# Memory tokens turned by VectorE's 32 by 32 transposes in place of TensorE's, with the memory weights' rows read in the order that this leaves

## What is computed

```python
def rms_norm(x, g):
    xf = x.astype(jnp.float32)
    y = xf * lax.rsqrt(jnp.mean(xf * xf, axis=-1, keepdims=True) + EPS)
    return (y * g.astype(jnp.float32)).astype(x.dtype)
...
        mem_n = rms_norm(mem, norm_mem_src[l])        # mem: 256 x 2048
...
    kv = (mem_n @ w_kv).reshape(b, m, 2, MEM_HEADS, MEM_HEAD_DIM)   # w_kv: 2048 x 1024
    k, v = kv[:, :, 0], kv[:, :, 1]
```

## Time and profile before

| | us |
|---|---|
| median of 3 runs | 1361.85 |
| lowest, highest | 1360.79, 1362.06 |
| span of the profiled execution | 1359.5 |
| PE busy | 1003.1 |
| DVE busy | 579.6 |
| ACT busy | 300.6 |
| POOL busy | 52.5 |

### The profile page before, as it was taken

How to read it: one execution, slowest core, us unless ns; L and a number is a source line. 1 busy time by engine, 2 the same in 40 slices (tenths; PEclk the granted TensorE clock), 3 DMA queues, 4 the chain that set the end, 5 groups by cost and what they waited for, 6 DMA issues and landing times.

```text
span 1359.5 us, 20738 instructions
## 1 busy us (share of the span) xinstructions
PE 1003.1 (74%) x8580; PEld 605.0 (45%) x8580; DVE 579.6 (43%) x1119; ACT 300.6 (22%) x521; POOL 52.5 (4%) x108
## 2 busy tenths in 40 slices
PE   8999999999999976566655566655566655566656
PEld 7888888888888532222222222222222222222222
DVE  5545566786557553223332223332223332223323
ACT  5654457664455200000000000000000000000002
POOL 1300001222000000000000000000000000000001
PEclk9999999999999998778777778787777787777879
DMA  7866663238878999999999999999999999999997
GB/s 245 276 194 184 174 177 122 101 128 261 292 272 304 354 429 420 434 432 430 432 432 432 432 432 432 432 432 432 432 432 432 432 432 432 432 432 432 432 424 294
DMA packets 71220, 481.15 MB, mean 354 GB/s; under 512 B 9543, under 2 KB 19917, under 8 KB 57998
## 3 DMA queue, kind: packets, MB, share of 16 engines
q1 hardware_dynamic: 70684, 478.22, 87.1%
q10 hardware_dynamic: 306, 2.11, 0.4%
q0 software_dynamic: 192, 0.31, 0.2%
HBM read 478.52 MB, written 2.10 MB: 354 GB/s over the span
## 4 chain that ended last, share of the span: by engine, by line
PE 51%; DMA 45%; SPq 1%; DVE 1%; issue 1%; ACT 0%; DVEq 0%; ACTq 0%
DMA gu<-in_w_up 41%; PE ps L1028 10%; PE ps L576 8%; PE ps L578 8%; PE ps L577 8%; PE ps L1083 5%; DMA down<-in_w_down 4%; PE ps L1007 2%; PE ps L1040 1%; PE ps L556 1%; PE ps L827 1%; PE ps L828 1%; PE ps L829 1%; PE ps L754 1%; SPq L441 0%
## 5 line engine op out<-in xcount | busy, mean ns | idle before, releaser
L1028 PE MATMUL ps<-gu,xe 128*32 128x256 f32 x3968 | 285.7, 452 | 305.1 <-DMA gu<-in_w_up 304.6
L2096 DVE TENSOR_TENSOR x_sum<-ps,x_sum 128x512 f32<-128x512 f32 x240 | 149.1, 684 | 508.6 <-PE ps L1040 508.6
L1028 PEld LDWEIGHTS ps<-gu,xe 128*32 128x32 f32 x3968 | 140.4, 129 | 468.4 <-DMA gu<-in_w_up 327.8
L1580 DVE TENSOR_TENSOR w_lo<-w_raw,w_hi 128x1024 fp32r<-128x1024 f32 (+1 forms) x137 | 164.9, 1209 | 122.5 <-ACT w_hi L1201 119.2
L576 PE MATMUL ps<-w_hi,a_hi 128*128 128x512 f32 (+1 forms) x468 | 183.7, 393 | 0.0
L577 PE MATMUL ps<-w_lo,a_hi 128*128 128x512 f32 (+1 forms) x468 | 179.8, 384 | 0.0
L578 PE MATMUL ps<-w_hi,a_lo 128*128 128x512 f32 (+1 forms) x460 | 176.9, 385 | 0.0
L1201 ACT ACTIVATE w_hi<-w_raw 128x1024 fp32r<-128x1024 f32 (+1 forms) x137 | 141.7, 1039 | 131.8 <-PE ps L578 116.1
L1499 ACT ACTIVATE sg<-ps 128x128 f32<-128x128 f32 x31 | 8.6, 278 | 654.5 <-PE ps L1028 654.5
L1083 PE MATMUL ps<-down,act_t 128*32 128x512 f32 x976 | 112.6, 602 | 6.2 <-DMA down<-in_w_down 6.2
L577 PEld LDWEIGHTS ps<-w_lo,a_hi 128*128 128x128 f32 x468 | 88.0, 188 | 16.4
(11 more groups left out here) (341 smaller groups left out, 866.0 us busy)
## 6 DMA issues: line engine op xcount, KB each, us to landing
down<-in_w_down SPq DMA_DIRECT2D x29, 4096.0 KB, 22.7
gu<-in_w_gate SPq DMA_DIRECT2D x28, 4096.0 KB, 31.6
gu<-in_w_up SPq DMA_DIRECT2D x28, 4096.0 KB, 40.9
w_raw<-in_w_in SPq DMA_DIRECT2D x56, 512.0 KB, 4.2
w_raw<-in_w_out SPq DMA_DIRECT2D x32, 512.0 KB, 4.4
gu<-in_w_up SPq DMA_DIRECT2D x18, 512.0 KB, 6.0
w_raw<-in_w_mem_kv SPq DMA_DIRECT2D x16, 512.0 KB, 3.4
down<-in_w_down SPq DMA_DIRECT2D x13, 512.0 KB, 15.3
```

Source lines behind the costliest of these rows:

```text
L1028: mm = pe.matmul(ps[5][j * SLOTS:(j + 1) * SLOTS, 0:2 * P].rearrange("s (m f) -> s m f", m=2), xe[:, k, :], gu[side][:, :, k, j * P:(j + 1 ...
L1580: ve.tensor_tensor(w_lo[:, u % RING, :, 0:n], w_raw[:, u % RING, :, 0:n], w_hi[:, u % RING, :, 0:n], ALU.subtract).then_inc(S("w_split"), 1)
L2096: ins = ve.tensor_tensor(x_sum[:, t, cols], ps[g][:, :], (x_res if first else x_sum)[:, t, cols], ALU.add)
```

## The change

- The tokens are loaded by four DMAs on ACT's queue, one for each quarter of the columns: partitions 32q to 32q+31 get columns 512q to 512q+511 of all 256 tokens, eight tokens per partition, in pieces of 2 KB (`mem_quads`).
- DVE transposes each of the eight 128 by 512 slices in place, as sixteen columns of 32 by 32 blocks whose elements lie 16 apart (64 bytes). Partition p then holds features 16p to 16p+15. Four of these instructions stand in chunk SB_V, four in SB_V + 1 (`turn_mem`).
- The unit loads of the memory weights read rows 16p + k on partition p, in pieces of 2 KB as before; the gain of the memory norm is loaded by a DMA of its own straight into `g_t` in that order, and the PE transpose of gains has 70 rows.
- PE's 32 transposes of `mem_sb` go. `a_hi` and `a_lo` are written by ACT and DVE from SBUF, reading with the 64-byte step (`mem_heads`, `mem_rest`).
- The squares become eight ACT instructions of 512 elements, four behind chunk SB_K and four behind SB_K + 1. POOL spreads them over a 128 by 256 tile with four added instructions (three small ones make `quad_eye`), PE sums across partitions with two matmuls of one column ahead of the latent chunks, DVE copies the sums out of PSUM, and POOL's norm of the memory moves ahead of the heads.
- The semaphore `counted` becomes a second count of `ranked`; other counts and gain columns are renumbered.

```diff
@@ load of the weights, of the gains
             if MEM_K <= c <= MEM_V:
-                return [cols(w_mem_kv, (c - MEM_K) * UN)]
+                return [w_mem_kv[0, :, (c - MEM_K) * UN:(c - MEM_K + 1) * UN].rearrange(
+                    "(p k) n -> p k n", k=KD)[:, i * UK:(i + 1) * UK, :]]
...
+                sp.dma_start(g_t[:, 70:86], norm_mem_src[0].rearrange("(p k) -> p k", k=KD)).then_inc(
+                    S("mem_loaded"), 16)
@@ tensor
             turn(KV_LAT)
             pe.wait_ge(S("turn_copied"), bank0[KV_LAT])
-            pe.wait_ge(S("mem_loaded"), 16)
+            pe.wait_ge(S("mem_spread"), 1)
+            for t in range(TT):
+                mm = pe.matmul(ps[7][:, t:t + 1], mem_spread[:, NJ * t:NJ * (t + 1), :].rearrange(
+                    "p j s -> p (j s)"), ones[:, 0:1], start=True, stop=True)
+            mm.then_inc(S("squares_summed"), 1)
             for n, (c, i) in enumerate(LATENT):
...
-                if n < KD // 2:
-                    split_turn("mem", mem_sb, 2 * n, 2 * n + 2)
@@ scalar
+            def mem_squares(t):
+
+                sc.wait_ge(S("mem_loaded"), 16 * (NJ + 1))
+                for j in range(NJ):
+                    square(mem_quads[:, NJ * t + j, :], chunk_ss[:, t, j:j + 1], mem_junk[:, :])
+                    sq[0] += 1
+                    sc.wait_ge(S("squared"), sq[0])
...
-                    sc.dma_start(mem_sb[:, :, :], mem[0].rearrange("(t p) d -> p t d", p=P)).then_inc(
-                        S("mem_loaded"), 16)
+                    for q in range(NJ):
+                        sc.dma_start(mem_quads[q * QUAD:(q + 1) * QUAD, :, :],
+                                     mem[0, :, q * UN:(q + 1) * UN].rearrange("(j s) f -> s j f", s=QUAD)
+                                     ).then_inc(S("mem_loaded"), 16)
...
+                if SB_K <= c < SB_V:
+                    mem_squares(c - SB_K)
                 if c == SB_K:
...
+            def mem_heads(k):
+
+                if k == 0:
+                    sc.wait_ge(S("w_used"), START[Q_PE])
+                    sc.wait_ge(S("split_turned"), (SPLIT0["mem"] + KD) // 2)
+                sc.activation(a_hi[:, k, :].rearrange("p (j s) -> p j s", s=QUAD), mem_turned[:, k], ACT.Copy,
+                              scale=g_t[:, 70 + k:71 + k]).then_inc(S("split_hi"), 1)
@@ vector
+            def turn_mem(t):
+
+                ve.wait_ge(S("squared"), 3 * TT + NJ * (t + 1))
+                for j in range(NJ * t, NJ * (t + 1)):
+                    tile = mem_quads[:, j, :].rearrange("p (r k) -> p k r", k=KD)
+                    ve.transpose(tile, tile).then_inc(S("split_turned"), 1)
+
             for c in range(Q_LAT, Q_PE):
                 split_w(DONE[c] + RING)
+                if c >= SB_V:
+                    turn_mem(c - SB_V)
...
+            ve.wait_ge(S("squares_summed"), 1)
+            ve.tensor_copy(sums[:, SS_MEM:SS_MEM + TT], ps[7][:, 0:TT]).then_inc(S("sums_made"), 1)
             for n, (c, i) in enumerate(LATENT):
                 split_w(POS[(c, i)] + RING)
                 if n < KD // 2:
-                    split_rest("mem", 16, k_from=2 * n, k_to=2 * n + 2)
+                    mem_rest(2 * n)
+                    mem_rest(2 * n + 1)
```

More of the change, by code:

```diff
@@ L36 @@
 SLOTS = 32
+QUAD = 32
 NJ = P // SLOTS
@@ L109 @@
         _b = len(SPLIT_BANK)
-        SPLIT_BANK.append(6 + _b % 2 if _name == "mem" else 4 + _b % 4)
+        SPLIT_BANK.append(None if _name == "mem" else 4 + _b % 4)
 def bank_before(b):
@@ L168, in layer @@
         g_nat_at = at[0]
-        g_nat = place("g_nat", [86, P])
+        g_nat = place("g_nat", [70, P])
         g_t = place("g_t", [P, 86])
@@ L201, in layer @@
         c_kv = place("c_kv", [P, TT, KV_RANK + ROPE])
-        mem_junk = place("mem_junk", [P, D], offset=km_at)
-        mem_sb = place("mem_sb", [P, TT, D], offset=o_at)
+        mem_junk = place("mem_junk", [P, UN], offset=km_at)
+        mem_spread = place("mem_spread", [P, TT * NJ, QUAD], offset=km_at + 2048)
+        quad_eye = place("quad_eye", [P, QUAD], offset=km_at + 3072)
+        mem_quads = place("mem_quads", [P, TT * NJ, UN], offset=o_at)
+        mem_turned = mem_quads[:, :, :].rearrange("p j (s k) -> p k j s", k=KD)
         cq_hi = place("cq_hi", [P, 4, SEQ], F32R, offset=k_at)
@@ L356, in load_small @@
             def load_small():
-                for gain, r0, rows in ((norm_mem_src, 16, 16), (norm_mem_x, 32, 16),
-                                       (norm_q_lat, 48, 4), (norm_kv_lat, 52, 2), (norm_mla_out, 54, 8),
-                                       (norm_sb_out, 62, 8), (norm_ffn, 70, 16)):
+                for gain, r0, rows in ((norm_mem_x, 16, 16), (norm_q_lat, 32, 4), (norm_kv_lat, 36, 2),
+                                       (norm_mla_out, 38, 8), (norm_sb_out, 46, 8), (norm_ffn, 54, 16)):
                     sp.dma_start(g_nat[r0:r0 + rows, :], gain[0].rearrange("(k p) -> k p", p=P)
                                  ).then_inc(S("gains_loaded"), 16)
+                sp.dma_start(g_t[:, 70:86], norm_mem_src[0].rearrange("(p k) -> p k", k=KD)).then_inc(
+                    S("mem_loaded"), 16)
                 for t in range(TT):
@@ L379, in early_piece @@
                     sp.wait_ge(S("out_lo"), KD)
-                    sp.wait_ge(S("sums_made"), 1)
+                    sp.wait_ge(S("sums_made"), 2)
                 if n < 8:
@@ L663, in _ @@
                 if i == 3:
-                    pe.wait_ge(S("gains_loaded"), 7 * 16)
-                    pe.transpose(ps[3][:, 0:86], g_nat[:, :], ident[0:86, 0:86]).then_inc(
+                    pe.wait_ge(S("gains_loaded"), 6 * 16)
+                    pe.transpose(ps[3][:, 0:70], g_nat[:, :], ident[0:70, 0:70]).then_inc(
                         S("gains_turned"), 1)
@@ L805, in _ @@
                 if q == 1:
-                    pe.wait_ge(S("sums_made"), 1)
+                    pe.wait_ge(S("sums_made"), 2)
                 split_turn("memx", x_res, 4 * (q - 1), 4 * q)
@@ L997, in rank_all @@
                 pe.matmul(ps[3][:, 0:EXPERTS], ones[:, :], sel[:, EXPERTS:TT * EXPERTS], start=False,
-                          stop=True).then_inc(S("counted"), 1)
+                          stop=True).then_inc(S("ranked"), 1)
             def gather(n):
@@ L1284, in _ @@
             sc.wait_ge(S("gains_turned"), 2)
-            sc.activation(g_t[:, 16:86], ps[3][:, 16:86], ACT.Copy).then_inc(S("gains_copied"), 1)
+            sc.activation(g_t[:, 16:70], ps[3][:, 16:70], ACT.Copy).then_inc(S("gains_copied"), 1)
             sc.wait_ge(S("gains_copied"), 2)
@@ L1319, in _ @@
                     chunk_copy(c, lambda t: v_sb[:, t, n0:n0 + UN], SS_X)
+                if SB_K <= c < SB_V:
+                    mem_squares(c - SB_K)
                 if c == SB_K:
-                    split_head("q", 48, hi=cq_hi)
+                    split_head("q", 32, hi=cq_hi)
                 if c == SB_K + 1:
[L1323 to L1328, removed]
+                    split_head("kv", 36, hi=ckv_hi)
+            def mem_heads(k):
[4 more added lines that the diff above has]
+                              scale=g_t[:, 70 + k:71 + k]).then_inc(S("split_hi"), 1)
             for n, (c, i) in enumerate(LATENT):
@@ L1332, in _ @@
                 if n < KD // 2:
-                    split_head("mem", 16, START[Q_PE], k_from=2 * n, k_to=2 * n + 2)
+                    mem_heads(2 * n)
+                    mem_heads(2 * n + 1)
                 if POS[(c, i)] + 1 < DONE[c]:
@@ L1685, in _ @@
                              ALU.max).then_inc(S("angles"), 1)
+            def turn_mem(t):
[3 more added lines that the diff above has]
+                    ve.transpose(tile, tile).then_inc(S("split_turned"), 1)
             for c in range(Q_LAT, Q_PE):
                 split_w(DONE[c] + RING)
+                if c >= SB_V:
+                    turn_mem(c - SB_V)
                 if c == SB_K + 1:
-                    split_rest("kv", 52, hi=ckv_hi, lo=ckv_lo)
+                    split_rest("kv", 36, hi=ckv_hi, lo=ckv_lo)
                 if SB_Q <= c - 1 < SB_V:
@@ L1692, in _ @@
                     if c == SB_K:
-                        split_rest("q", 48, hi=cq_hi, lo=cq_lo)
+                        split_rest("q", 32, hi=cq_hi, lo=cq_lo)
                     if c - 1 == SB_K + 1:
@@ L1706, in _, with mem_rest @@
             copy_turned(KV_LAT)
+            def mem_rest(k):
+                ve.wait_ge(S("split_hi"), SPLIT0["mem"] + k + 1)
+                ve.scalar_tensor_tensor(
+                    out=a_lo[:, k, :].rearrange("p (j s) -> p j s", s=QUAD), in0=mem_turned[:, k],
+                    scalar=g_t[:, 70 + k:71 + k],
+                    in1=a_hi[:, k, :].rearrange("p (j s) -> p j s", s=QUAD), op0=ALU.mult,
+                    op1=ALU.subtract).then_inc(S("split_lo"), 1)
+            ve.wait_ge(S("squares_summed"), 1)
+            ve.tensor_copy(sums[:, SS_MEM:SS_MEM + TT], ps[7][:, 0:TT]).then_inc(S("sums_made"), 1)
```

(21 more changed lines are left out.)

20 lines of the change are left out of this document (7 added, 13 removed).

## The result

The changed kernel is **slower**: 1362.84 us (median of 20 runs) against 1360.56 us of the kernel before in the same series, ratio 1.0017 with a 95% interval of 1.0011 to 1.0023. That is 2.3 us more, where 2.65 less was forecast; the time lies outside the stated range. The difference is 0.17%, clear of noise but under the 0.2% that the prediction took as the least it could tell from no change.

What follows compares the result with a forecast made beforehand. PE was taken to bound the kernel until about 474 us, then mostly DMAs of expert weights. Span 1359.5 - 3.1 + 0.45 = 1356.85, with the median 2.35 higher, gave 1359.2 us; 8-in-10 range 1358.2 to 1361.2.

Steps and rivals of the forecast that it cites:

- the early load: Four token DMAs from 53 us, landing by 89 us, first read at 116.6 us: nothing, up to 0.5 us lost.
- The cushion I took from ACT's roundings: Behind the early load's issue: three more issues, 1.2 us on ACT, against three weight units of 2.72 us each.
- PE's gain: Latent chunks: removed transposes save 3.5 us, two one-column matmuls cost 0.4 us; 3.1 us less if PE is never starved.
- The transposes: DVE in SB_V and SB_V + 1: 1.07 us each from a stepped write, four in 3.9 us, or 2.5 to 5.3.
- ACT's and DVE's stepped reads: After SB_V + 1's transposes: two heads 0.73 us, `mem_rest` as before or 0.18 more; PE waits 0.45 us at Q_NOPE + 1.
- rival 1: Step halves DVE and ACT rates: transposes 1.25 us, PE waits 1.9 us, net gain 1.2, 1360.65 us; chance 0.25.
- the later latent units: Weight units after the Q_NOPE + 1 wait: 1 to 4 us in hand when the queues are carried on.
- The base of the time: Span of 1359.5 us for the kernel before, with the runs' median 2.35 us above the profiled span.
- "The same": Outcome of no measurable change, within some 0.2% or 2.7 us; chance 0.53 from part of the forecast plus rivals 1 and 3.
- SB_K, SB_V, POOL, the carry to the end: Squares 3.0 us per chunk and SB_V's transposes hidden, POOL nothing; PE savings before 474 us move everything behind.
- The memory weights' rows: Memory weight loads, same bytes and 2 KB pieces, read where DMA engines are two to three tenths busy; counted within early load.
- The rival on the other side: Rival 2, slower: in-place stepped transposes far slower, starving SB_V and SB_V + 1; at 2 us each, 1366 us; chance 0.08.

Runs made afterwards that it cites:

- the three kernels with the whole change: The changed kernel (1362.84 us), the same with transposes one chunk earlier (1360.22 us), and the same with densely written transposes (1360.94 us), all with the change's original load.
- every fourth partition: Kernel before, its token load cut into four DMAs of 8 KB rows, each to 32 partitions taken every fourth; 1360.47 us, ratio 1.0002.
- copy first: Changed kernel with spread loads, earlier transposes and dense write, ACT copying both Q_NOPE chunks' banks before its next rounding and heads; 1357.79 us, ratio 0.9978.
- the dense-write runs: Transposes write densely into the next slot: on the changed kernel alone 1360.94 us; with spread loads and earlier transposes 1358.49 and 1358.59 us.

## Why the prediction was wrong

- **The step that failed: the early load at "nothing, up to 0.5 us lost".** I asked when the tokens would have to be there (116 us, true: they were) and not what the load does to the transfers beside it. It cost 2.1 us by itself and 1.7 to 2.8 in the three kernels with the whole change. The rows to ask were at hand: the DMA engines' slices at six to eight tenths in the first 100 us, against a ring that holds four units. The cushion I took from ACT's roundings, three units, is a cushion for ACT, not for a transfer of 13.6 us. The issues themselves, 1.9 us more on ACT instead of 1.2, were hidden: every fourth partition issues four at one point too and loses nothing.
- **PE's gain, 3.5 us less 0.4.** Right: with every wait in it mended (copy first), the latent stage is 3.10 us shorter than before. The two small matmuls took 0.45.
- **The transposes.** Forecast 1.07 us each, measured 1.076, four in 4.00. The number was right by luck: I put the extra down to the write, and the dense-write runs show that the write's step costs nothing. The first row that spoke against a read cost, line 2084, reads PSUM.
- **ACT's and DVE's stepped reads.** DVE's 0.68 instead of 0.48 us was the upper bound named. For ACT the sum took the old 0.73 per pair; measured 1.29 and 1.31. This term of the sum was mis-sized by 1.1 us over the two pairs before the split. The wait that came of it all was 1.5 us where 0.45 was forecast; rival 1 had 1.9, and its price for a pair of heads, 1.1, was nearer.
- **The bank at K_NOPE + 1** was not in the working, which gave the later latent units 1 to 4 us in hand: the removed transposes had given ACT the time for its copy. 0.4 us when everything else is mended, 0.9 in the changed kernel.
- **The base of the time.** The sum started from three runs with a median of 1361.85; twenty put the same kernel at 1360.56. A run's time lies 1.7 to 1.8 us above its span wherever both are on record, so the 2.35 us held a difference between executions too. The same 2.65 us off the twenty runs' median is 1357.9: the forecast time was 1.3 us too high for its own terms, and the miss is larger than 1362.84 against 1359.2 shows. "The same", which had chance 0.53, is where 0.17% falls by the prediction's own line, but not by any path that it named. (In the first of the 13 slices PE stands at eight tenths, not nine; nothing hangs on it.)
- **SB_K, SB_V, POOL, the carry to the end**: as forecast. ACT's 3 us of squares are hidden, no PE wait falls in SB_V + 1, and the lateness at 212.7 (2.7 us) arrives at the end as 2.4.
- **The memory weights' rows** read 16 apart: median 3.7 us to land instead of 3.4, hidden.

In sum: -3.05 on PE, +1.7 at Q_NOPE + 1 and +0.9 at K_NOPE + 1 (the gaps between matmuls, less what they are without a wait) make -0.4 in the latent stage; +0.3 before the load and +2.8 by the load in this profile; 2.7, measured 2.4 in the spans and 2.3 in the medians. With the 2.1 us that the load costs by itself the sum is 1.7, inside the interval of the ratio (1.5 to 3.1 us). The rival on the other side had the wrong place: not the transposes, but the load.

## What to carry to other kernels

Work that leaves the critical engine leaves its cushions too: price what the replaced instructions gave time to, and price a transfer by what it does to those that share the engines at that moment, not only by when it must land. A load that must go to 32 neighbouring partitions and shares the DMA engines with a short ring is worth spreading in time: some 12 to 14 us apart, the four cost nothing here. Where VectorE or ScalarE must read with a step, let it be done once, by an instruction that has room, and written densely for the readers behind it. And measure a stretch from an instruction of its own, not from the start of the span.

## What the runs showed of the hardware

- DMAs to 32 neighbouring partitions moved 224 GB/s with the weight loads beside them, those to every fourth partition 367, at the same share of busy DMA engines (1.00 and 0.99). The same 2.10 MB took 34% of the engines' time from 50 to 78 us in the first and 21% in the second.
- A transpose of 128 by 512 took 0.717 us from PSUM with a step of 64 bytes and 1.08 us from SBUF with the same step, whether its write was dense or not. The Trainium skill, page SBUF — State Buffer, section Door 1, says that SBUF is read in lines of 16 bytes and that float32 may step by up to four elements for free; the SBUF figures here agree. Of PSUM it says only that non-contiguous access slows matmuls; for VectorE's transpose no cost of the step shows.
- The same step in SBUF cost ScalarE 0.26 us on 256 elements (0.768 against 0.504) and VectorE 0.20 (0.676 against 0.478).
